# Products of 64 channels issued for two heads in turn, and pooling's outputs moved in ScalarE's order

## The chip, the cores and the metric

One core of a Trainium2 chip runs the whole program. The metric is the device time of one execution in microseconds (us), the median of three runs. A time differs from the profile's span by what lies around the span. The engines are TensorE (PE in the profile; its weight loads are PEld), VectorE (DVE), ScalarE (ACT), GpSimd (POOL) and SyncE (SP), which here only issues weight loads.

## The reference, cut to what matters

A sequence of 512 tokens with 1024 channels passes two hybrid layers (attention and retention), a feed-forward block, a token mixer, another feed-forward block and a last norm, all in fp32. The change lies in the token mixer. It has four groups of 256 channels: pooling, two gated linear attentions (`hgrn` and `gla`) and an RWKV-7 recurrence, the last three with four heads of 64 channels:

```
o = einsum('bhts,bhsv->bhtv', scores, vc) + (q * exp(b)) @ S        # hgrn, gla, per head
S_t = S_{t-1} diag(w_t) - (S_{t-1} kk_t)(kk_t * a_t)^T + v_t k_t^T  # rwkv, per head
y_pool = (window means - p) @ w_pool                                # 64 channels per window
```

## The kernel before, in words

Each engine has its own program, written out by hand in one order (`tensor_engine`, `vector_engine`, `scalar_engine`, `gpsimd_engine`, `sync_engine`). They meet through semaphores: `p.up(name, ...)` signals, `wait_ge(*of(name, ...))` waits. An engine runs its queue strictly in order, so a waiting instruction holds all that is behind it.

Features lie on partitions. The channels of head h are rows 0 to 63 (h even) or 64 to 127 (h odd) of feature tile h // 2 (`head_tile`). A product over one head's 64 channels thus has 64 rows on one half of TensorE's array: for each of four token tiles (`TT`), a 64x128 stationary and a 64x128 moving operand give a 128x128 block of one PSUM bank. TensorE takes the eight banks in turn (`take`), and waits until the reader of what was last in a bank has released it; a bank in `held` is passed over.

**Linear attention** (`linear_attention`, for `hgrn`, then `gla`). VectorE sums the log decays ("decay summed"). TensorE makes the near products k2 x q2 for the four heads, masked by VectorE. Then come nine levels in `ORDER` (32, 16, 8, 4, 2, 1, 64, 128, 256): VectorE makes log factors, ScalarE exponentials (`factor`), VectorE factors, TensorE score products (`scores`). Up to level 64 these products go by both row halves in turn already (L789). For 128 and 256 they were issued head by head, and ScalarE evicts them ("far"). Between the levels `fill(n)` issues work that doesn't depend on them: projections by weight units, whose halves ScalarE (`w_high`) and VectorE (`w_low`) split ahead of use.

**Pooling.** GpSimd makes the windows; TensorE's four pooling products are in `fill(0)` of `hgrn`. ScalarE evicts them to `y_pool`, in its own `fill(0)`, behind two weight splits. ScalarE's order was `factor(0)`, then `fill(0)`. Four banks are held by the `hgrn` values at that time, so the near products go to the four banks that pooling's outputs leave.

**The RWKV inverse** (`inverse`). When the operands are ready ("rE"), `gram` makes for each head the products AT (bI x kkE) and X (kkE x bI). Between them stand `bonus_sums` (products with 2 moving columns, into one held bank) and `turn_operands` (transposes of a token tile). VectorE masks AT and copies into XT and X, then runs `finish_gla`, the norm of gla's output, whose root ScalarE takes ahead of its inverse work. Then the inverse doubles its blocks over sizes 2, 4, 8, 16 and 32: Pm = CT x X for each head (CT by GpSimd), evicted by ScalarE, then `updates`, added to X and XT by VectorE. Between them three slots for each size take a step of `side_products`: A_ak, M_rk, M_rb (`gram` again, masked by VectorE) and Gv = A_ak x values (evicted by ScalarE). `side_products` exists on TensorE, VectorE and ScalarE, and the three must agree in their steps.

`keep_busy` issues unread products on TensorE ahead of some waits. An fp32 product stands in the trace as two records, so sixteen products are x32. Many small products go through the helper `group` and so have line L432.

## Time and profile before

| | us |
|---|---|
| three runs | 1779.49, 1781.59, 1781.84 |
| median | 1781.59 |
| profiled execution, its own time | 1780.97 |
| span of that execution | 1779.2 |
| mean granted clock over the span | 0.98 |
| mixer part up to the end of the inverse | about 960 to 1311 of the span |

The profile is of one execution. Engines are "busy" while an instruction runs; the end of a matmul is modelled and contains a tail, so the spacing of starts tells more than a duration. PEclk is the granted clock of TensorE as a share of full speed, 2.4 GHz; 0.50 is its lower level, 1.2 GHz. In brackets behind a row stands how long the engine had been idle and what released it.

### The profile page before, as it was taken

How to read it: one execution, taken by the hardware profiler on the slowest of the kernel's cores; microseconds unless marked ns; L12 is line 12 of the kernel's file. 1: busy time of each engine (PE TensorE's matmuls, PEld its weight loads, DVE VectorE, ACT ScalarE, POOL GpSimd, SP SyncE). 2: the span in 40 equal slices, each digit the busy share in tenths (PEclk: the TensorE clock that was granted, in tenths of full speed). 3: DMA queues.
4: the chain of work that ended last, by engine and by line, in shares of the span. 5: the costliest groups of instructions: out<-in, count | busy, mean ns of one | idle time of the engine just before them, and what ended most of it. 6: DMA issues, size and time to landing. Idle time of an engine off the chain costs nothing.

```text
span 1779.2 us, 22284 instructions
## 1 busy us (share of the span) xinstructions
PE 1716.0 (96%) x8770; PEld 1396.2 (78%) x8770; DVE 875.6 (49%) x1169; ACT 675.5 (38%) x1017; POOL 129.3 (7%) x126
## 2 busy tenths in 40 slices
PE   7999999999999899999999899989998899999997
PEld 6777778878778788888888688868987688888886
DVE  5633445633445565444334676765345554444333
ACT  5145564225555333333223553463132433333221
POOL 0001002001000100000002200001320200000000
PEclk9999999999999999999999899987999999999998
DMA  5422213322212233233333222100011223223331
GB/s 187 129 71 72 83 48 97 120 92 84 71 61 73 70 107 95 95 100 96 96 96 134 71 63 68 60 19 1 1 30 36 83 90 100 95 98 96 91 98 57
DMA packets 40745, 143.92 MB, mean 81 GB/s; under 512 B 4816, under 2 KB 4832, under 8 KB 40384
## 3 DMA queue, kind: packets, MB, share of 16 engines
q1 hardware_dynamic: 37008, 130.87, 22.9%
q0 software_dynamic: 2192, 8.73, 1.6%
q10 hardware_dynamic: 1440, 2.88, 0.4%
q8 instruction: 70, 1.15, 0.3%
q14 instruction: 35, 0.29, 0.1%
HBM read 140.37 MB, written 2.10 MB: 80 GB/s over the span
## 4 chain that ended last, share of the span: by engine, by line
PE 84%; DVE 10%; ACT 4%; issue 1%; DMA 0%; POOL 0%; DVEq 0%; ACTq 0%; SPq 0%
PE bank L450 23%; PE bank L451 22%; PE bank L452 22%; PE bank L432 8%; PE bank L438 2%; DVE sb_w_low L1133 2%; PE bank L789 1%; DVE sb_rot L1133 1%; PE bank L668 1%; PE bank L647 1%; PE bank L604 1%; DVE sb_xg_low L1141 1%; ACT sb_w_high L1872 1%; DVE sb_x L1133 1%; PE bank L527 0%
## 5 line engine op out<-in xcount | busy, mean ns | idle before, releaser
L1133 DVE TENSOR_TENSOR sb_w_low<-sb_raw,sb_w_high 128x1024 fp32r<-128x1024 f32 (+1 forms) x253 | 310.0, 1225 | 390.0 <-ACT sb_w_high L1872 384.0
L450 PE MATMUL bank<-sb_xg_high,sb_w_high 128*128 128x512 f32 x1176 | 468.1, 398 | 23.5 <-DVE sb_xg_low L1141 15.6
L451 PE MATMUL bank<-sb_xg_low,sb_w_high 128*128 128x512 f32 x1176 | 460.8, 392 | 0.0
L452 PE MATMUL bank<-sb_xg_high,sb_w_low 128*128 128x512 f32 x1176 | 460.8, 392 | 0.0
L1872 ACT ACTIVATE sb_w_high<-sb_raw 128x1024 fp32r<-128x1024 f32 (+1 forms) x253 | 263.4, 1041 | 354.7 <-PE bank L452 324.2
L450 PEld LDWEIGHTS bank<-sb_xg_high,sb_w_high 128*128 128x128 f32 x1176 | 222.4, 189 | 89.2 <-issue 31.0
L452 PEld LDWEIGHTS bank<-sb_xg_high,sb_w_low 128*128 128x128 f32 x1176 | 222.4, 189 | 47.7
L451 PEld LDWEIGHTS bank<-sb_xg_low,sb_w_high 128*128 128x128 f32 x1176 | 222.6, 189 | 44.3
L452 PE MATMUL bank<-sb_h_high,sb_w_low 128*128 128x512 f32 x352 | 136.9, 389 | 0.0
L450 PE MATMUL bank<-sb_h_high,sb_w_high 128*128 128x512 f32 x352 | 136.9, 389 | 0.0
L451 PE MATMUL bank<-sb_h_low,sb_w_high 128*128 128x512 f32 x352 | 136.9, 389 | 0.0
L2440 POOL TENSOR_TENSOR sb_square_sum<-sb_square_sum,sb_square 128x512 f32<-128x512 f32 x34 | 45.3, 1333 | 958.3 <-ACT sb_square L1872 882.2
L450 PE MATMUL bank<-sb_w_high,sb_xg_high 128*128 128x512 f32 x256 | 103.9, 406 | 0.5 <-DVE sb_w_low L1133 0.4
L451 PE MATMUL bank<-sb_w_low,sb_xg_high 128*128 128x512 f32 x256 | 100.6, 393 | 0.0
L452 PE MATMUL bank<-sb_w_high,sb_xg_low 128*128 128x512 f32 x256 | 100.3, 392 | 0.0
L451 PEld LDWEIGHTS bank<-sb_h_low,sb_w_high 128*128 128x128 f32 x352 | 66.1, 188 | 13.8
L452 PEld LDWEIGHTS bank<-sb_h_high,sb_w_low 128*128 128x128 f32 x352 | 66.1, 188 | 13.8
L450 PEld LDWEIGHTS bank<-sb_h_high,sb_w_high 128*128 128x128 f32 x352 | 66.1, 188 | 13.5
L1872 ACT ACTIVATE sb_h_high<-sb_up 128x512 fp32r<-128x512 f32 x44 | 27.8, 633 | 118.4 <-DVE sb_up L1133 118.4
L1133 DVE TENSOR_TENSOR sb_up<-bank,sb_inv_rms 128x512 f32<-128x512 f32 x44 | 30.4, 692 | 81.2 <-PE bank L452 80.6
L1872 ACT ACTIVATE sb_gate<-sb_gate 128x512 f32<-128x512 f32 x44 | 27.8, 633 | 95.2 <-DVE sb_gate L1133 95.2
L450 PEld LDWEIGHTS bank<-sb_w_high,sb_xg_high 128*128 128x128 f32 x256 | 48.5, 189 | 19.2 <-issue 8.2
(336 smaller groups left out, 2110.1 us busy)
## 6 DMA issues: line engine op xcount, KB each, us to landing
sb_raw<-w_ffn_in SPq DMA_DIRECT2D x88, 512.0 KB, 3.3
sb_raw<-w_ffn_out SPq DMA_DIRECT2D x32, 512.0 KB, 3.5
sb_raw<-w_tok SPq DMA_DIRECT2D x24, 512.0 KB, 3.9
sb_raw<-w_mix_f SPq DMA_DIRECT2D x18, 512.0 KB, 3.3
sb_raw<-w_rot SPq DMA_DIRECT2D x16, 512.0 KB, 3.7
sb_raw<-w_qk SPq DMA_DIRECT2D x16, 512.0 KB, 3.3
sb_raw<-w_out SPq DMA_DIRECT2D x16, 512.0 KB, 3.3
sb_raw<-w_ffn_out SPq DMA_DIRECT2D x16, 384.0 KB, 3.1
```

The lines of the kernel that those rows point to most:

```text
L432: made = e.matmul(out, lhsT, rhs, start=n == 0, stop=n == len(pairs) - 1)
L438: made = e.transpose(banks[i][:, blk(n)], in_, mem.ident)
L450: e.matmul(out, w[0], v[0], start=first, stop=False)
L451: e.matmul(out, w[0], v[1], start=False, stop=False)
L452: return e.matmul(out, w[1], v[0], start=False, stop=last)
L604: made = e.matmul(out[k], m.feat["rk"][r, f, blk(j)], m.feat["rq"][r, f, j * P:], start=part == 0, stop=part == 1)
L647: e.matmul(out[k], m.qT[r, j, blk(q)], m.kT[r, j, 0:keys], start=True, stop=True).then_inc(*p.up("scores", n, 2 * j + k, q))
L668: made = e.matmul(out[64 * k:64 * k + 64, blk(q)], m.tok["av"][:, key, h * ATT_DIM:(h + 1) * ATT_DIM], m.probT[:, 2 * (q % 2) + k, blk(key ...
L789: made = e.matmul(banks[i][:, at:at + 64].rearrange("p (n c) -> p n c", c=size), et, halves(et, size, True), start=True, stop=True)
L1133: e.tensor_tensor(out, a, b, op).then_inc(*v.up(*signal))
L1872: e.activation(out, in_, func, bias=bias, scale=scale, accum_out=accum).then_inc(*a.up(*signal))
L2440: e.tensor_tensor(out, a, b, op).then_inc(*g.up(*signal))
```

## The change

TensorE's products over one head's 64 channels are issued for two heads in turn (`HEAD_PAIRS`), one on the upper and one on the lower rows, each into its own bank; both banks are taken first. That holds for the near products, the far levels 128 and 256, and all of `gram`. In the entry to the inverse the order becomes AT of two heads, two bonus sums, X of two heads, two bonus sums, two turns. The side products get five steps for two heads (ten in all) instead of three for one (twelve in all), on all three engines. On ScalarE `hgrn`'s `fill(0)` goes ahead of `factor(0)`.

```diff
 # TensorE, linear_attention
             fill(0)
-            for h in HEADS:
-                r, g = head_tile(h)
-                i = take(("near", name, h), ("near", name, h))
-                p.wait_ge(*of("decay summed", name, 1))
+            p.wait_ge(*of("decay summed", name, 1))
+            for two in HEAD_PAIRS:
+                out = [take(("near", name, h), ("near", name, h)) for h in two]
                 for t in range(TT):
-                    group(banks[i][:, blk(t)], [(k2[r, g, blk(t)], q2[r, g, blk(t)])], "near product", name, h)
+                    for h, i in zip(two, out):
+                        r, g = head_tile(h)
+                        made = e.matmul(banks[i][:, blk(t)], k2[r, g, blk(t)], q2[r, g, blk(t)], start=True, stop=True)
+                        if t == TT - 1:
+                            made.then_inc(*p.up("near product", name, h))
...
-                    for h in HEADS:
-                        r, g = head_tile(h)
-                        i = take(("pairs", name, n, h), ("far", name, n, h))
...
+                    for two in HEAD_PAIRS:
+                        out = [take(("pairs", name, n, h), ("far", name, n, h)) for h in two]
+                        for k in range(2):
+                            for h, i in zip(two, out):
...
 # TensorE, inverse
-        def gram(what, h, left, right):
+        def gram(what, two, left, right):
...
             for t in range(TT):
-                group(banks[i][:, blk(t)], [(left[r, f, blk(t)], right[r, f, blk(t)])], what + " product", h)
+                for h, i in zip(two, out):
+                    r, f = head_tile(h)
+                    made = e.matmul(banks[i][:, blk(t)], left[r, f, blk(t)], right[r, f, blk(t)], start=True, stop=True)
...
-        for h in HEADS:
-            gram("AT", h, m.bI, m.kkE)
-            if h < 2:
-                bonus_sums(2 * h)
-            gram("X", h, m.kkE, m.bI)
-            if h < 2:
-                bonus_sums(2 * h + 1)
-            if h:
-                turn_operands(h - 1)
-        turn_operands(3)
+        for two in HEAD_PAIRS:
+            gram("AT", two, m.bI, m.kkE)
+            if not two[0]:
+                bonus_sums(0)
+                bonus_sums(1)
+            gram("X", two, m.kkE, m.bI)
+            if not two[0]:
+                bonus_sums(2)
+                bonus_sums(3)
+            for t in two:
+                turn_operands(t)
...
+            for two in HEAD_PAIRS:
+                gram("A_ak", two, m.kI, m.kkE)
+                yield
+                for h in two:
...
+                    per_tile(("Gv product", h), ("Gv", h), tile_of(m.A_ak[:, h % 2, :]),
+                             lambda t: m_tokB(t, v_cols), cols64)
+                    yield
+                gram("M_rk", two, m.kI, m.rE)
+                yield
+                gram("M_rb", two, m.bI, m.rE)
                 yield
 # ScalarE, linear_attention
-            factor(0)
-            fill(0)
+            if name == "hgrn":
+                fill(0)
+                factor(0)
+            else:
+                factor(0)
+                fill(0)
```

## Rows read from the trace of the kernel before

**Rows 1.** The page, section 1: busy time, share of the span, number of records
```profile
PE 1716.0 (96%) x8770; PEld 1396.2 (78%) x8770; DVE 875.6 (49%) x1169; ACT 675.5 (38%) x1017; POOL 129.3 (7%) x126
```

**Rows 2.** Windows by stage: stretch, length, busy (records) by engine, PEclk, DMA share, GB/s
```profile
1012.18:1024.61 12.43, 12.43 (x56) 10.52 (x57) 8.30 (x10) 4.44 (x5) 0.00 (x0) 0.65 0.31 92
...
1024.61:1167.97 143.36, 143.35 (x997) 119.48 (x996) 102.06 (x114) 65.64 (x75) 0.00 (x0) 1.00 0.20 64
...
1208.98:1232.68 23.70, 23.70 (x112) 21.85 (x113) 11.01 (x14) 5.41 (x10) 2.54 (x2) 0.57 0.00 0
...
1236.03:1311.28 75.25, 75.25 (x625) 71.83 (x625) 28.34 (x53) 14.43 (x27) 29.99 (x24) 1.00 0.00 1
```

**Rows 3.** Timeline, TensorE, pooling's products to hgrn's second scores: start, us, form, xrecords [wait]
```profile
1003.28 1.93 PE L432 MATMUL bank<-sb_window,sb_pool_w 64*64 64x512 f32 x8
...
1012.18 5.13 PE L432 MATMUL bank<-sb_kq_hgrn 64*128 64x128 f32 x32 [6.97 <-ACT sb_y_pool L1872]
...
1024.61 2.00 PE L789 MATMUL bank<-sb_E 64*128 64x64 f32 x32
...
1032.21 2.00 PE L789 MATMUL bank<-sb_E 64*128 64x64 f32 x32
```

**Rows 4.** Timeline, TensorE: hgrn's far, gla's near, lora, and gla's far products
```profile
1079.80 3.74 PE L432 MATMUL bank<-sb_E 64*128 64x128 f32 x32
...
1109.03 2.82 PE L432 MATMUL bank<-sb_kq_gla 64*128 64x128 f32 x32
...
1170.93 3.65 PE L432 MATMUL bank<-sb_mixed,sb_lora 64*128 64x512 f32 x8 [2.94 <-ACT sb_mixed L1872]
...
1191.87 1.99 PE L432 MATMUL bank<-sb_E 64*128 64x256 f32 x12 [1.26 <-DVE sb_bI L1141]
```

**Rows 5.** Timeline, ScalarE, from the logarithms to the y_pool evictions
```profile
1002.60 1.28 ACT L1872 ACT_TABLE_LOAD   x1
...
1007.84 1.06 ACT L1872 ACTIVATE sb_E<-sb_E 128x1024 f32<-128x1024 f32 x1 [3.95 <-DVE sb_E L1133]
...
1011.35 3.38 ACT L1872 ACTIVATE sb_y_pool<-bank,sb_small,sb_cols 64x512 f32<-64x512 f32 x4
```

**Rows 6.** Timeline, VectorE, same stretch: decay sums, first log factors, two splits
```profile
1003.87 2.48 DVE L1153 TENSOR_TENSOR_SCAN sb_c_hgrn<-sb_mixer,sb_c_hgrn 128x512 f32<-128x512 f32 x2
...
1006.39 1.42 DVE L1133 TENSOR_TENSOR sb_E<-sb_c_hgrn 128x512 f32<-128x512 f32 x2
...
1010.10 2.56 DVE L1133 TENSOR_TENSOR sb_w_low<-sb_raw,sb_w_high 128x1024 fp32r<-128x1024 f32 x2 [2.29 <-ACT sb_w_high L1872]
```

**Rows 7.** Timeline, TensorE, inverse: a side product block and the update behind it
```profile
1241.58 1.16 PE L432 MATMUL bank<-sb_kkE,sb_kI 64*128 64x128 f32 x8
...
1242.66 1.11 PE L432 MATMUL bank<-sb_Pm,sb_XT 128*128 128x64 f32 x8
```

**Rows 8.** Timeline, entry to the inverse: bonus products, VectorE, ScalarE's root, first update
```profile
1210.07 0.61 PE L432 MATMUL bank<-sb_mixer,sb_sigma 128*128 128x2 f32 x4
...
1210.46 0.69 DVE L1133 TENSOR_TENSOR sb_AT<-bank,sb_mixer 128x512 f32<-128x512 f32 x1 [1.53 <-ACT sb_XT L1872]
...
1211.18 0.73 DVE L1719 COPY_PREDICATED sb_XT<-sb_mixer,bank 128x512 f32<-128x512 int32 x1
...
1230.27 1.23 DVE L1133 TENSOR_TENSOR sb_square<-sb_y_gla 128x1024 f32<-128x1024 f32 x1
...
1231.53 1.22 DVE L1149 TENSOR_REDUCE sb_small<-sb_square 128x16 f32<-128x1024 f32 x1
...
1235.07 0.22 ACT L1872 ACTIVATE sb_small<-sb_small 128x16 f32<-128x16 f32 x1
...
1236.03 1.11 PE L432 MATMUL bank<-sb_Pm,sb_XT 128*128 128x64 f32 x8 [1.39 <-ACT sb_Pm L1872]
```

**Rows 9.** Windows, as rows 2, of the entry to the inverse at low clock
```profile
1212.08:1229.32 17.24, 17.24 (x74) 15.65 (x74) 6.42 (x9) 2.39 (x4) 1.87 (x2) 0.50 0.00 0
...
1229.32:1232.56 3.24, 3.24 (x16) 3.24 (x16) 2.99 (x3) 1.58 (x3) 0.00 (x0) 0.50 0.00 0
```

More of the change, by code:

```diff
@@ L39 @@
 HEADS = range(4)
+HEAD_PAIRS = ((0, 1), (2, 3))
 LAYERS = 2
@@ L793, in scores @@
                 else:
-                    for h in HEADS:
-                        r, g = head_tile(h)
-                        i = take(("pairs", name, n, h), ("far", name, n, h))
-                        if size == 128:
-                            for k, key in enumerate((0, 2)):
-                                group(banks[i][:, blk(k)], [(x2[r, g, blk(key)], x2[r, g, blk(key + 1)])],
-                                      "pairs", name, n, h)
-                        else:
-                            for key in range(2):
-                                group(banks[i][:, key * 256:(key + 1) * 256],
-                                      [(x2[r, g, blk(key)], x2[r, g, 256:512])], "pairs", name, n, h)
+                    for two in HEAD_PAIRS:
+                        out = [take(("pairs", name, n, h), ("far", name, n, h)) for h in two]
+                        for k in range(2):
+                            for h, i in zip(two, out):
+                                r, g = head_tile(h)
+                                if size == 128:
+                                    made = e.matmul(banks[i][:, blk(k)], x2[r, g, blk(2 * k)], x2[r, g, blk(2 * k + 1)],
+                                                    start=True, stop=True)
+                                else:
+                                    made = e.matmul(banks[i][:, k * 256:(k + 1) * 256], x2[r, g, blk(k)],
+                                                    x2[r, g, 256:512], start=True, stop=True)
+                                if k:
+                                    made.then_inc(*p.up("pairs", name, n, h))
                 p.mark("factors read", name, n)
@@ L923, in inverse @@
         before_products = ("rE",)
-        def gram(what, h, left, right):
-            r, f = head_tile(h)
-            i = take((what, h), {"AT": ("XT made", 2, h), "X": ("X made", 2, h)}.get(what, (what, h)))
+        def gram(what, two, left, right):
+            out = [take((what, h), {"AT": ("XT made", 2, h), "X": ("X made", 2, h)}.get(what, (what, h))) for h in two]
             p.wait_ge(*of(*before_products))
             for t in range(TT):
-                group(banks[i][:, blk(t)], [(left[r, f, blk(t)], right[r, f, blk(t)])], what + " product", h)
+                for h, i in zip(two, out):
+                    r, f = head_tile(h)
+                    made = e.matmul(banks[i][:, blk(t)], left[r, f, blk(t)], right[r, f, blk(t)], start=True, stop=True)
+                    if t == TT - 1:
+                        made.then_inc(*p.up(what + " product", h))
         def per_tile(key, freed_by, left, right, out):
@@ L1729, in side_products @@
         def side_products():
-            for h in HEADS:
-                if h >= 2:
-                    v.wait_ge(*of("Gv product", h - 2))
-                masked("A_ak", m.A_ak[:, h % 2, :], h, mem.table("before"))
+            for two in HEAD_PAIRS:
+                for h in two:
+                    if h >= 2:
+                        v.wait_ge(*of("Gv product", h - 2))
+                    masked("A_ak", m.A_ak[:, h % 2, :], h, mem.table("before"))
                 yield
-                masked("M_rk", m.M_rk[:, h, :], h, mem.table("upto"))
                 yield
-                masked("M_rb", m.M_rb[:, h, :], h, mem.table("upto"))
+                yield
+                for h in two:
+                    masked("M_rk", m.M_rk[:, h, :], h, mem.table("upto"))
+                yield
+                for h in two:
+                    masked("M_rb", m.M_rb[:, h, :], h, mem.table("upto"))
                 yield
@@ L2151, in scores @@
                     act(m.far[:, h, at], bank("pairs", name, n, h)[:, 0:at.stop - at.start], "far", name, n, h)
[L2153 to L2154 removed]
+            if name == "hgrn":
+                fill(0)
+                factor(0)
+            else:
+                factor(0)
+                fill(0)
             for n in range(len(ORDER)):
@@ L2321, in side_products @@
         def side_products():
-            for h in HEADS:
+            for two in HEAD_PAIRS:
                 yield
-                a.wait_ge(*of("Gv product", h))
-                a.wait_ge(*of("y made", "gla"))
-                act(m.Gv[:, h, :], bank("Gv product", h)[:, 0:TT * 64], "Gv", h)
+                for h in two:
+                    a.wait_ge(*of("Gv product", h))
+                    a.wait_ge(*of("y made", "gla"))
+                    act(m.Gv[:, h, :], bank("Gv product", h)[:, 0:TT * 64], "Gv", h)
+                    yield
                 yield
```

11 lines of the change are left out of this document (3 added, 8 removed).

## The prediction

> **What bounds the kernel now.** The page first: TensorE is busy 1716.0 us of 1779.2 [rows 1], so time can be won only where TensorE's own work gets shorter, where it waits, or where its clock is low. The change touches the mixer part alone, so I cut that part into stages [rows 2]. TensorE is busy for 143.35 of 143.36 us between the first score products of hgrn and the last of gla; it is bound by its own work there, and what comes out of it, or ahead of it, comes off the end. The entry to the inverse (1208.98 to 1232.68) is also full of matmuls, at a mean clock of 0.57; the inverse behind it runs at 1.00 without a gap. The stretch before the first scores (to 1024.61) has 0.65.
>
> The timeline of TensorE says why: behind pooling's products it stands idle for 6.97 us, released by ScalarE's eviction of y_pool, and the 16 near products of hgrn then take 5.13 us [rows 3], where gla's 16 of the same shape take 2.75 [rows 4]. ScalarE's queue gives the reason for the wait: table load, then an exponential that waits for VectorE until 1007.84, then two weight splits in the 2.45 us before 1011.35, and only there the y_pool evictions [rows 5], though pooling's products began at 1003.28.
>
> **Part 1, pooling ahead of the exponents.** The change puts two splits and four evictions ahead of the first exponential on ScalarE. Their inputs are there: the logarithms end at about 1002.5 (the load starts then). The two splits fill at most 2.45 us: to 1004.9. Evictions at 3.38/4 = 0.85 each: the second ends at 1006.6, the fourth at 1008.3. The near products of heads 0 and 1 now take two banks at once, so they need the second eviction, and the decay sums, which end at 1006.35 [rows 6]. They start at 1006.6 and take 1.0; heads 2 and 3 go from 1008.3 to 1009.3. Behind them TensorE needs the next weight unit. VectorE's low halves wait behind its first log factors (1006.39 + 1.42), then 1.28 for the first: 1009.1. So the unit starts at 1009.3, where it started at 1017.3. At full clock a unit takes 5.6 us (the score products at 1024.61 and 1032.21 stand 7.6 apart, with 2.0 of their own and one unit between [rows 3]), and the scores would begin at 1014.9.
>
> What is queued behind: the table load (1.28) now falls after the evictions, the exponential ends at 1010.7 instead of 1008.9, VectorE's factors at 1012.0, its near copies after that. None is late for scores at 1014.9. SP only sees its weight loads released about a microsecond earlier; POOL has no part. The DMA queues are at 0.20 share there [rows 2].
>
> The clock: it fell in the 6.97 us wait. Now the waits are 1.3 and 0.7 us, but around them stand only pooling's quarter-array products and a microsecond of near products. I expect a short fall all the same, for most of a unit: nearly what the unit lost before (7.3 us from 1017.3 to 1024.6, against 5.6), 1.5 us; bounds 0 and 3.5. Part 1 gives 1024.61 - 1014.9 - 1.5 = **8.2 us** (6.2 to 9.7).
>
> **Part 2, two heads in turn.** No row shows these products alternated at 128 columns, so I bound one pair. From above: 16 products of 64 rows with 64 moving columns, already alternated (L789), take 2.00 us [rows 3]: 0.25 a pair, loads of 128 stationary columns included. Also alternated are four lora products of 512 columns, at half clock: 3.65 us [rows 4]. hgrn's near products at that clock take 5.13/13 = 0.39 for 128 columns, so one of 512 needs 1.6 and four in a row 6.3: two and two ran together. From below: gla's near products, four at a time on one row half, take 2.75/13 = 0.21 each if each of the three changes of half hides one product (2.75 is to the next start; the row's 2.82 has the tail). A pair at 0.21 to 0.25 costs what one product costs now. The worst end is no gain (rival 2).
> Here the Trainium skill speaks against the change: "TensorE: Matmul & The Clock Gate", Part 3, says that a weight load overlaps running matmuls only if the row group differs. By it a half would load, stream, then load again, 0.43 a pair, and the sum below would lose nearly all of part 2. The trace disagrees: four products of one half follow each other in 1.08 us [rows 7], 0.27 each, not 0.43, so the sum does not use it.
>
> Priced so:
> - gla's near products: 2.75 to 1.9, gain **0.8**; TensorE-bound, so all of it counts.
> - hgrn's far products: 8 of 128 and 8 of 256 columns take 3.66 us to the next start (the row of rows 4 merges both sizes and has the tail); four pairs of each take 0.85 + 1.7 + 0.4 for starts = 2.95: gain **0.7**.
> - gla's far products: heads 0 and 1 now both wait for the bank that VectorE frees at 1191.87 [rows 4]; ScalarE's four evictions then come in a row instead of one early, and the exponentials behind them are on VectorE's path to rE: about half an eviction of the length in rows 5, loss **0.4**.
> - inverse side products: 12 blocks of 1.08 become 6 [rows 7]. **Gain 6.5**, if no wait takes their place. With none of them, VectorE, ScalarE and POOL must keep up with products and updates alone; the stage is 38% VectorE, 19% ScalarE, 40% POOL [rows 2], and two heads in turn give each copy at least one block of TensorE's time. I take no wait; bound 2 us lost.
>
> **Part 3, the entry to the inverse.** Before, from first product (1208.98) to the first update (1236.03) [rows 8] is 27.05 us. After, at full clock: AT of two heads 1.1, four bonus products 1.0 (two take 0.54), X of two heads 1.1, bonus 1.0, two turns of operands 1.8 (16 transposes took 3.24 at half clock [rows 9]), AT 1.1, X 1.1, turns 1.8: TensorE is through after 10 us. So the cover is gone and the wait changes hands. VectorE needs per head a mask (0.72) and two predicated copies (0.84 with the step to the next) [rows 8]. AT of heads 2 and 3 is there at 7.4 us; VectorE finishes six operations 4.8 us later, at 12.2; then finish_gla's squares and reduction (1.26 each) to 14.7; ScalarE's root, which is ahead of Pm in its queue, starts at 15.0, its table load done earlier; the first update followed the root's start by 0.96 [rows 8], with Pm of head 0 between: 16.0, say 16.1. The first Pm product also waits, since seven banks turn round, for the XT copy of head 3 at 11.4. The stage takes 16.1 instead of 27.05: gain 10.9, less 0.5 for a chance of a low clock during the bonus products: **10.4**.
>
> **The price of it.** TensorE now stands idle for about 1.3 and then 2.8 us with 1.9 us of work between. In the trace a wait of 6.97 us cost the clock, and so did plain thin work: it fell in this very stage, with no wait, and stayed at 0.50 for 17.24 us of one-half products and transposes; it came back only at the end of 3.24 us of nothing but transposes [rows 9]. So I expect the inverse to begin at 1.2 GHz. It came back behind the transposes, and behind the alternated lora products of rows 4. The nearest to these in the inverse is a Pm product next to a pair of side products (3.7 us at half clock), or two Pm products. The first such stretch comes after updates of two heads and a product (3.5 + 1.8 + 3.5 us), so the half clock lasts about 12 us and costs **6** (0 if it never falls; 13 if the first stretch misses).
>
> **Sum.** 8.2 + 0.8 + 0.7 - 0.4 + 6.5 + 10.4 - 6 = 20.2 us. The profiled execution took 1780.97 us for its span of 1779.2; that gives 1760.8. The median of the runs is 0.6 higher, 1761.4. The last term has its tail on the dear side, so I say 1762. Terms at their good ends: 9.7 + 1.1 + 6.5 + 10.9 = 28.2, or 1753. At their bad ends: 6.2 + 1.1 + 4.5 + 9.5 - 13 = 8.3, or 1773.
>
> **Rivals.**
> 1. The clock holds through the entry, or comes back at once. For it: the pairs fill both halves of the array, where the trace fell on one-half products. Against: the 2.8 us wait. Sum without the last term, 26.2: 1755. Chance 0.15.
> 2. The change doesn't do what it says: pairs don't overlap at 128 columns, because each half waits for its own loads. Then part 1 gives 8.2, part 2 nothing, and part 3, with products as long and a clock as low as now, little: 1773. For it: the four products of rows 7 take 1.08, a little over 4 x 0.21. Against: rows 3 and 4. Chance 0.05. (This is what the page's rule above would give.)
> 3. The low clock stays for 25 to 45 us of the inverse, since most of it is 64-column updates that wait on loads: cost 13 to 22, time 1768 to 1777. For it: the 17 us at 0.50. Against: the stretch is at 1.00 now with the same updates. Chance 0.15.
> 4. Slower: the low clock lasts through the inverse. Its place is the idle before the first update; about 69 us of work would take 69 more, 26.2 is won elsewhere: 1824. It decides from 52 us of half clock on, where the cost (half the time) passes 26.2. Against it: two stretches like that in each of five sizes. Chance 0.03.
> The forecast itself: 0.62.
>
> **Chances.** A measurement of this kernel can tell about 0.2%, 3.6 us, from no change. Faster by more than that needs a time under 1778: forecast, rivals 1 and 2, nearly all of 3: 0.94. Between: the rest of 3 and a bad rival 2: 0.03. Slower: 0.03. The range that holds 8 in 10 leaves out rival 4, the slow part of 3 and the fastest of 1: 1752 to 1773.
>
> **What would show it.** hgrn's near products beginning 3.3 us after pooling's first product instead of 8.9, the table load behind y_pool; gla's 16 near products in about 1.9 us; side blocks of 16 records in 1.1 to 1.2 us, six of them; a first update 16 us after the first AT product with VectorE and ScalarE, not TensorE, before it; and a granted clock below 1 for the first 12 us of the inverse. Wrong if a pair costs more than 0.3 us, if the Pm evictions begin to hold TensorE in the inverse, or if the clock in the inverse is low for more than one size.

## The result, and the profile after

The changed kernel took 1755.63 us, median of four runs (1755.07 to 1756.98), beside 1780.54 for the kernel before on the same chip (1779.12 to 1781.84). The ratio is 0.9861, 95% interval 0.9844 to 0.9878. The forecast was 1762, range 1752 to 1773. The profiled execution took 1755.07 us for a span of 1753.3.

The starts of the same work on TensorE in both traces give the account. "Foretold" is the prediction's own term, all numbers are us.

| TensorE reaches | before | after | won in the step | foretold |
|---|---|---|---|---|
| pooling's products | 1003.28 | 1003.27 | 0.0 | 0 |
| hgrn's first scores | 1024.61 | 1016.94 | 7.7 | 8.2 |
| hgrn's far products | 1079.80 | 1073.68 | -1.6 | 0 |
| gla's near products | 1109.03 | 1102.96 | -0.1 | 0.7 |
| gla's last 64-channel scores | 1164.20 | 1157.66 | 0.5 | 0.8 |
| first AT product | 1208.98 | 1203.08 | -0.6 | -0.4 |
| first update | 1236.03 | 1218.81 | 11.3 | 10.4 |
| end of the inverse | 1311.28 | 1288.31 | 5.8 | 6.5 - 6 |
| end of the recurrence | 1384.65 | 1358.71 | 3.0 | 0 |
| end of the span | 1779.2 | 1753.3 | 0.0 | 0 |

The sum won is 25.9 us against 20.2 foretold. Two places make the difference: the inverse (5.8 for 0.5) and the recurrence (3.0 for nothing). These are two single executions, and that of the changed kernel is the fastest of its four; by the medians the change is worth 24.9 us in this set and 22.4 in a second set further down.

The page's first section, which answers to [rows 1], shows where it went: TensorE's busy time fell by 22.7 us, on the same number of records.

```profile
PE 1693.3 (97%) x8770; PEld 1377.0 (79%) x8770; DVE 875.3 (50%) x1169; ACT 674.9 (38%) x1017; POOL 129.9 (7%) x126
```

**Ahead of the first scores.** ScalarE's timeline, which answers to [rows 5]:

```profile
1002.78 2.23 ACT L1891 ACTIVATE sb_w_high<-sb_raw 128x1024 fp32r<-128x1024 f32 x2
1005.12 3.37 ACT L1891 ACTIVATE sb_y_pool<-bank,sb_small,sb_cols 64x512 f32<-64x512 f32 x4
1008.57 1.28 ACT L1891 ACT_TABLE_LOAD   x1
1009.87 1.06 ACT L1891 ACTIVATE sb_E<-sb_E 128x1024 f32<-128x1024 f32 x1
```

TensorE's timeline beside it, which answers to [rows 3] (rows left out are weight-unit products):

```profile
1003.27 1.93 PE L433 MATMUL bank<-sb_window,sb_pool_w 64*64 64x512 f32 x8
1006.91 1.16 PE L780 MATMUL bank<-sb_kq_hgrn 64*128 64x128 f32 x16 [1.70 <-ACT sb_y_pool L1891]
1008.64 1.73 PE L780 MATMUL bank<-sb_kq_hgrn 64*128 64x128 f32 x16 [0.57 <-ACT sb_y_pool L1891]
1010.31 0.79 PE L451 MATMUL bank<-sb_w_high,sb_xg_high 128*128 128x512 f32 x1
...
1016.94 0.55 PE L793 MATMUL bank<-sb_E 64*128 64x64 f32 x6
```

The wait of 6.97 us is now 1.70 and 0.57. The second block of the same form takes 1.73 us where the first took 1.16: the clock fell within it, and the first row of the weight unit, 0.79 (0.50 for the first row of the next unit, at full clock), shows it low still. The last row shown is cut by the end of the view: it is the start of 32 records.

**The entry to the inverse.** Rows that answer to [rows 8], TensorE first:

```profile
1203.08 1.16 PE L938 MATMUL bank<-sb_kkE,sb_bI 64*128 64x128 f32 x16 [0.19 <-DVE sb_rE L1147]
1204.18 1.05 PE L433 MATMUL bank<-sb_mixer,sb_sigma 128*128 128x2 f32 x8
1205.16 1.16 PE L938 MATMUL bank<-sb_bI,sb_kkE 64*128 64x128 f32 x16
1206.25 1.05 PE L433 MATMUL bank<-sb_mixer,sb_sigma 128*128 128x2 f32 x8
...
1214.18 2.02 PE L433 MATMUL bank<-sb_X,sb_CT 128*128 128x128 f32 x16 [1.19 <-DVE sb_XT L1733]
1218.81 1.11 PE L433 MATMUL bank<-sb_Pm,sb_XT 128*128 128x64 f32 x8 [2.60 <-ACT sb_Pm L1891]
```

VectorE's timeline from the last XT copy on, then ScalarE's up to the first Pm evictions:

```profile
1213.31 0.72 DVE L1733 COPY_PREDICATED sb_XT<-sb_mixer,bank 128x512 f32<-128x512 int32 x1
...
1215.34 1.22 DVE L1147 TENSOR_TENSOR sb_square<-sb_y_gla 128x1024 f32<-128x1024 f32 x1
1216.59 1.22 DVE L1163 TENSOR_REDUCE sb_small<-sb_square 128x16 f32<-128x1024 f32 x1
```
```profile
1217.85 0.22 ACT L1891 ACTIVATE sb_small<-sb_small 128x16 f32<-128x16 f32 x1 [1.89 <-DVE sb_small L1163]
1218.15 1.28 ACT L1891 ACTIVATE sb_Pm<-bank 128x512 f32<-128x512 f32 x2
```

This is the hand-over that the prediction drew: TensorE is through with the operands after 10 us, and then the bank of head 3's XT, VectorE's reduction, ScalarE's root and the Pm eviction behind it set the first update.

How much of the 11.3 us is what? Windows over the entry of before, then of after (columns as in [rows 2]):

```profile
1208.98:1236.03 27.05, 25.65 (x129) 23.61 (x129) 11.76 (x16) 8.39 (x15) 4.58 (x4) 0.62 0.00 1
```
```profile
1203.08:1218.81 15.73, 11.94 (x129) 10.99 (x129) 11.81 (x16) 8.39 (x15) 5.80 (x4) 1.00 0.01 2
```

At a mean clock of 0.62, 27.05 x 0.38 = 10.3 us of before's busy time were the price of the clock. Without it TensorE had 15.4 us of work; now it has 11.9. Waits rose from 1.4 to 3.8. So 11.3 = 10.3 (clock) + 3.4 (shorter work) - 2.4 (more waiting). By this account the gain is nearly all clock. The two traces don't say which part of the change kept the clock up, the alternation or the new order of the blocks; the experiment with the alternation undone bears on it.

**The inverse.** A side block of two heads, which answers to [rows 7], on TensorE's timeline; then windows over the whole inverse [rows 2] and over its one low stretch:

```profile
1225.99 1.16 PE L938 MATMUL bank<-sb_kkE,sb_kI 64*128 64x128 f32 x16
```
```profile
1218.81:1288.31 69.50, 69.50 (x624) 67.25 (x624) 28.13 (x53) 14.41 (x27) 29.80 (x24) 0.98 0.01 1
...
1220.70:1224.10 3.40, 3.40 (x18) 3.40 (x17) 1.68 (x3) 0.60 (x1) 1.27 (x1) 0.50 0.00 0
```

Eight products of two heads, alternated, take 1.09 us to the next start; four of one head took 1.08. TensorE is busy all through; no eviction took the place of the work removed. The half clock that I expected for 12 us lasted 3.4.

### The profile page after: what moved, and what is told of

Same layout as the page of the kernel before. It is cut to its first block, busy times and chain, and to the rows that moved or that the text cites. A ratio compares the mean times of both kernels' runs of the same rounds, so it can differ in the third digit from the quotient of the medians.

```text
span 1753.3 us, 22293 instructions
## 1 busy us (share of the span) xinstructions
PE 1693.3 (97%) x8770; PEld 1377.0 (79%) x8770; DVE 875.3 (50%) x1169; ACT 674.9 (38%) x1017; POOL 129.9 (7%) x126
## 4 chain that ended last, share of the span: by engine, by line
PE 81%; DVE 12%; ACT 5%; issue 1%; DMA 0%; POOL 0%; DVEq 0%; ACTq 0%; SPq 0%
PE bank L451 23%; PE bank L452 22%; PE bank L453 22%; PE bank L433 6%; DVE sb_w_low L1147 2%; PE bank L439 2%; ACT sb_w_high L1891 1%; PE bank L669 1%; PE bank L648 1%; PE bank L605 1%; DVE sb_xg_low L1155 1%; DVE sb_E L1147 1%; PE bank L793 1%; DVE sb_x L1147 1%; DVE sb_rot L1147 1%
## 5 line engine op out<-in xcount | busy, mean ns | idle before, releaser
L451 PE MATMUL bank<-sb_xg_high,sb_w_high 128*128 128x512 f32 x1176 | 469.1, 399 | 23.8 <-DVE sb_xg_low L1155 15.4
L451 PEld LDWEIGHTS bank<-sb_h_high,sb_w_high 128*128 128x128 f32 x352 | 66.1, 188 | 13.7
L452 PEld LDWEIGHTS bank<-sb_h_low,sb_w_high 128*128 128x128 f32 x352 | 66.1, 188 | 13.7
L453 PEld LDWEIGHTS bank<-sb_h_high,sb_w_low 128*128 128x128 f32 x352 | 66.1, 188 | 13.7
```

The costliest lines, as they stand in the source:

```text
L451: e.matmul(out, w[0], v[0], start=first, stop=False)
L452: e.matmul(out, w[0], v[1], start=False, stop=False)
L453: return e.matmul(out, w[1], v[0], start=False, stop=last)
```

## The experiments

Times are medians. Where kernels ran with the same "before" they are named together.

### Pooling's order alone, and the pairs alone

The first is the kernel before with only ScalarE's order changed, the second the changed kernel with only that undone:

```diff
-            factor(0)
-            fill(0)
+            if name == "hgrn":
+                fill(0)
+                factor(0)
+            else:
+                factor(0)
+                fill(0)
```

> The kernel before with only ScalarE's order changed (hgrn's fill(0) ahead of factor(0)). Theory (the first near products waited only for the y_pool evictions, and the wait cost the clock): the first score products of hgrn start 7 to 8 us earlier than before, near 1017, and the whole is 7 to 9 us shorter than before, 1772 to 1774. Rival A (the wait only changes hands, to the weight split or the exponential): first scores after 1022, whole within 3 us of before.

> The changed kernel with ScalarE's old order. Theory (the two parts add up): 7 to 8 us above the changed kernel, 1762 to 1764. Rival A (the order gives nothing once products alternate): within 2 us of the changed kernel, 1754 to 1758.

Measured: 1770.89 (1768.77 to 1772.38) and 1760.12 (1759.37 to 1762.32), before 1778.85; ratios 0.9958 (0.9943 to 0.9973) and 0.9897 (0.9881 to 0.9914). TensorE, near products of hgrn, of the order alone, then of the pairs alone:

```profile
1006.39 3.96 PE L432 MATMUL bank<-sb_kq_hgrn 64*128 64x128 f32 x32 [1.28 <-DVE sb_c_hgrn L1153]
```
```profile
1013.59 0.80 PE L780 MATMUL bank<-sb_kq_hgrn 64*128 64x128 f32 x4 [7.85 <-ACT sb_y_pool L1891]
```

By the medians the order is worth 8.0 us by itself. By head, only the first bank is needed, so the products start on the decay sums (1.28), not on the second eviction. Without it the pairs wait 7.85 us, 0.9 more than before, because two evictions must be done. The two parts sum to 8.0 + 18.7 = 26.7 against 24.9 and 22.4 for both in the two sets of the changed kernel. That is 2 to 4 us too much, and the second expectation missed by as much: the pairs alone lie 4.5 and 3.4 us above the two sets, not 7 to 8. The starts on TensorE are steadier than the medians. From pooling's products to the first AT product the kernel before takes 205.7 us and the order alone 199.4, so the order wins 6.3 there; the pairs alone take 206.5 and the changed kernel 199.8, so it wins 6.7 on top of the pairs. In that stretch the two parts add up. (The first expectation had 7 to 8 us for it and 1772 to 1774 for the whole; the first scores came 6.4 us earlier, at 1018.24, and the median is 1.1 below the range.) The rest of the medians lies where the order changes nothing: the trace of the order alone has no low clock in the recurrence, where that of the kernel before has two stretches of 3.4 us.

### Alternation undone, order kept

Each block still holds two heads, but head by head. The cut shows `gram`; the near and the far products are edited in the same way:

```diff
-            for t in range(TT):
-                for h, i in zip(two, out):
-                    r, f = head_tile(h)
+            for h, i in zip(two, out):
+                r, f = head_tile(h)
+                for t in range(TT):
```

> The changed kernel with the same blocks, banks and steps, but in each block all products of one head, then all of the other. Theory (two products on different row halves run at the same time): each side block of 16 records takes 1.9 to 2.1 us instead of 1.09, six of them 5 to 6 us; the near products together 1 us more; the entry to the inverse falls to the low clock or at least takes 4 to 8 us longer. Whole 1767 to 1772. Rival B (the gain is in the grouping: fewer changes between half-row and full-row products, fewer steps): within 3 us of the changed kernel.

Measured: 1774.04, ten runs from 1761.65 to 1776.35, before 1778.85; ratio 0.996 (0.9938 to 0.9981). The profiled run is the fastest of the ten. Its timeline on TensorE, gla's near products and a side block:

```profile
1103.08 2.88 PE L780 MATMUL bank<-sb_kq_gla 64*128 64x128 f32 x32
1105.89 0.50 PE L451 MATMUL bank<-sb_w_high,sb_xg_high 128*128 128x512 f32 x1
...
1231.84 1.71 PE L938 MATMUL bank<-sb_kkE,sb_kI 64*128 64x128 f32 x16
1233.48 0.33 PE L433 MATMUL bank<-sb_Pm,sb_XT 128*128 128x64 f32 x1
```

A side block of two heads takes 1.64 us by head, 1.09 alternated, and two blocks of one head took 2 x 1.08. So of the 1.07 us that a merged block saves, half (0.55) is alternation and half (0.52) is one block less to start and end. The expectation had 1.9 to 2.1 us for the block, which would have left almost nothing to this second half. That also prices products of one row half at 1.64/8 = 0.21 when they run on, as the prediction had from gla's near products.

The profiled run is 6.6 us above the changed kernel's. The shorter products account for about 6 of that: 0.55 for each of the six side blocks, as much at most for each of the four entry blocks, and 0.5 for gla's near products. That the rest is so small is luck of two traces: this one loses 1.7 us more to the clock in the entry and as much in the inverse, and wins 2.6 behind the recurrence, where the changed kernel's clock falls once more. The other nine runs lie up to 14.7 us above that, at a mean granted clock down to 0.976 where the fastest run has 0.988. The longer runs have the lower clock, so with the products by head it is low longer in most executions. Where, I can't show: the trace is of the fastest run. Alternation is thus worth about 6 us in products and, by the medians (18.4 us apart), some 12 more, which go with the clock.

The same trace says something of the entry to the inverse. Its window, from the first AT product to the first update:

```profile
1204.57:1223.03 18.46, 15.44 (x129) 14.50 (x129) 11.77 (x16) 8.39 (x15) 5.78 (x4) 0.91 0.00 1
```

The clock is low for 3.4 us there, not for the 20.5 us of the kernel before, and the entry takes 18.5 us, not 27.05: in this execution 8.6 of the 11.3 us came with the new order of the blocks alone. The order alone on ScalarE, whose entry is as before, has the 20.5 us again. So in the entry it was not the alternation that kept most of the clock, at least in the fastest of these ten runs. What it does in the other nine is open, and no run has the old order of blocks with alternated products.

### The far levels by head

```diff
-                    for two in HEAD_PAIRS:
-                        out = [take(("pairs", name, n, h), ("far", name, n, h)) for h in two]
...
+                    for h in HEADS:
+                        r, g = head_tile(h)
+                        i = take(("pairs", name, n, h), ("far", name, n, h))
...
```

> The changed kernel with only the levels 128 and 256 issued head by head again. Theory (there, taking two banks ahead makes TensorE wait for ScalarE's evictions, 0.59 us in hgrn, and delays the exponentials of rwkv by 0.3 us in gla, which gives back what alternating won): hgrn's far products take 3.6 to 3.8 us as in the changed kernel, the whole is within 1 us of it, 1754.6 to 1756.2. Rival C (alternating them is worth 0.7 us or more): 1756.5 or above.

Measured: 1764.73 (1755.11 to 1766.58), before 1778.85; ratio 0.9913 (0.9884 to 0.9943). TensorE, hgrn's far products, by head:

```profile
1071.43 3.74 PE L433 MATMUL bank<-sb_E 64*128 64x128 f32 x32
1075.10 0.50 PE L451 MATMUL bank<-sb_w_high,sb_xg_high 128*128 128x512 f32 x1
```

and of the changed kernel, TensorE, then ScalarE's four evictions of level 128 (0.45 us each; the second ends just before TensorE goes on at 1075.43):

```profile
1073.68 1.16 PE L804 MATMUL bank<-sb_E 64*128 64x128 f32 x16
1075.43 2.08 PE L807 MATMUL bank<-sb_E 64*128 64x256 f32 x16 [0.59 <-ACT sb_far L1891]
1077.44 0.50 PE L451 MATMUL bank<-sb_w_high,sb_xg_high 128*128 128x512 f32 x1
```
```profile
1074.42 1.81 ACT L1891 ACTIVATE sb_far<-bank 128x256 f32<-128x256 f32 x4 [1.58 <-PE bank L804]
```

3.67 us by head, 3.76 in pairs: no gain. Both banks are taken before the first product of a pair, and the bank comes free only with ScalarE's eviction; the 0.59 us wait eats what the pairs save.

In gla the pairs even lose. From the lora products to the first AT product it is 38.0 us by head (here, in the kernel before and in the order alone) and 38.6 in pairs (in both traces of the changed kernel, in the pairs alone and in three more; in the remaining five the clock falls once more at about 1185, and it is 39.4 to 39.7). So the far levels are better left by head, by 0.6 us.

The expectation of the whole, within 1 us of the changed kernel, missed by 8. The 9 us that the median is above the changed kernel's do not come from there: counted from pooling's products the first AT product comes 0.7 us earlier than in the changed kernel's trace. The windows behind the first update, which stands at 1217.62, show what happened instead:

```profile
1218.00:1245.50 27.50, 27.50 (x137) 27.05 (x137) 7.03 (x13) 3.41 (x7) 5.07 (x4) 0.50 0.00 1
1245.50:1288.00 42.50, 42.50 (x405) 41.45 (x405) 17.74 (x36) 8.53 (x15) 15.24 (x12) 1.00 0.01 1
```

About 27.4 us at half clock, 13.7 lost, on the same code that lost 1.7 in the changed kernel's trace. This is the mechanism of rival 3, met in another kernel, behind the same 2.60 us wait for Pm. Whether the far levels by head have a part in it is open; one of its four runs took 1755.11, as the changed kernel.

### The changed kernel again, and the two waits of the entry taken away

Unchanged; then ScalarE's root behind the first two Pm evictions:

```diff
-        finish_gla()
...
+            if size == 2:
+                finish_gla()
```

then also the turn of the banks moved on by three behind the bonus sums, so that the first Pm product meets a bank that is free:

```diff
+        turn[0] += 3
```

> The changed kernel itself, more executions. Theory (the 2.6 us wait before the first update leaves the clock low in the inverse, and how long it stays low differs from execution to execution): times in two groups, some at 1753 to 1757, some 6 to 12 us above, at a lower mean clock. Rival D (only the form of the far products made the slow executions of the fourth run): all within 1754 to 1758.

> The changed kernel with ScalarE's finish_gla (table load and root) behind its first two Pm evictions instead of ahead of them. Theory (the first update waits for Pm of head 0, which waits in ScalarE's queue for the root and so for VectorE): the wait before the first update falls from 2.6 us to under 1, the first update comes about 13.3 us after the first AT product instead of 15.7; the low clock in the inverse gets rarer. Median 1750 to 1754. Rival E (something else holds the first update, the XT copies or a bank): first update still after 15 us or more, time as the changed kernel.

> As the run before, and TensorE passes over three banks ahead of the first Pm product, so that this takes a bank that ScalarE has emptied and not the one that waits for the XT copy of head 3. Theory: the 1.2 us wait ahead of the first Pm product goes too, first update about 12 us after the first AT product, no wait over 1 us is left in the entry and the clock holds there. Median 1749 to 1752, hardly any execution above 1755. Rival F (the X and XT copies on VectorE then hold the updates themselves): the gain over the run before is under 0.5 us.

> The kernel with the root behind the first Pm evictions and the bank turn moved on by three, once more. Its earlier four runs lay from 1748.8 to 1758.2 and those of the changed kernel from 1752.7 to 1761.9. Theory (two waits, 3.8 us together, are gone from the entry, nothing else is changed but the luck of the clock): median 1750 to 1754, first update 12.3 us behind the first AT product, as before. Rival (the lower median of the earlier runs was luck, the time is set behind the entry): 1755 to 1758, no different from the changed kernel.

Measured: changed again 1756.75 (1752.66 to 1761.88); root moved 1754.29 (1746.74 to 1757.96); root and bank 1751.09 (1748.81 to 1758.18), before 1779.15, ratios 0.9875 (0.9858 to 0.9893), 0.9858 (0.9837 to 0.9878) and 0.9849 (0.983 to 0.9868). Root and bank again: 1752.47 (1751.13 to 1757.81), before 1778.23, ratio 0.9855 (0.9828 to 0.9882). TensorE's first update with the root moved, then with both:

```profile
1214.14 2.02 PE L433 MATMUL bank<-sb_X,sb_CT 128*128 128x128 f32 x16 [1.20 <-DVE sb_XT L1733]
1216.00 1.06 PE L433 MATMUL bank<-sb_Pm,sb_XT 128*128 128x64 f32 x8
```
```profile
1211.31 1.95 PE L433 MATMUL bank<-sb_X,sb_CT 128*128 128x128 f32 x16
1213.83 1.11 PE L433 MATMUL bank<-sb_Pm,sb_XT 128*128 128x64 f32 x8 [0.57 <-ACT sb_Pm L1892]
```

From the first AT product (1203.04 and 1201.56) that is 12.96 and 12.27 us (12.27 again in the repeated set), against 15.73. Rivals E and F are out: both waits were where the prediction put them, the root costs 2.8 us, the bank 0.7. Of the 3.5 us about that much arrives in the median: all eight runs of the changed kernel have the median 1755.98, the eight of root and bank 1752.25 (on different chips, their kernels before within 2.3 us). The groups overlap, and so do the intervals, so this version is probably, not surely, better than the changed kernel; it beats the kernel before by 28.1 and 25.8 us in its two sets.

The expectations on the clock did less well. The changed kernel's second set has one run at 1761.88 and three from 1752.66 to 1757.28: rival D, all within 1754 to 1758, is out, so times above that don't need the far products by head, but one run is no group. With the root moved the low clock did not get rarer: three of the four traces that have it, without a filled wait, show 10.2 us at half clock in the inverse, where both traces of the changed kernel show 3.4. And "hardly any execution above 1755" missed: one of four is at 1758 in each set of root and bank.

### Unread products in the waits

The changed kernel with three unread products behind the first Pm products, where TensorE waits 2.60 us:

```diff
             product(0)
             product(1)
+            if size == 2:
+                keep_busy(3)
```

> The changed kernel with three unread products of 512 columns on TensorE in its 2.6 us wait before the first update; nothing else moves. Theory (it is the idle time that costs the clock): the granted clock stays at 1.00 through the inverse, no execution is above 1757, median 1752 to 1755. Rival G (the thin work behind the wait brings the clock down whatever stands in the wait): low clock in the inverse as before, executions at 1761 to 1767 remain.

Measured: 1753.70 (1751.30 to 1755.03, five runs), before 1779.15; ratio 0.9854 (0.9841 to 0.9868). TensorE's timeline at that place, and the window over the inverse:

```profile
1214.79 2.74 PE L751 MATMUL bank<-sb_inv_rms,sb_ones 128*128 128x512 f32 x6
1217.56 1.11 PE L433 MATMUL bank<-sb_Pm,sb_XT 128*128 128x64 f32 x8
```
```profile
1215.00:1287.00 72.00, 71.98 (x644) 67.95 (x643) 31.57 (x59) 15.89 (x31) 32.55 (x25) 1.00 0.01 1
```

The clock stays at 1.00 over the whole inverse, and the spread is 3.7 us, against 9.2 in the changed kernel's second set. But its first set of four had spread over only 1.9, so the spread says little. The clear sign is the clock behind this wait: low in all six traces that have the 2.60 us idle, not low here. That fits the idle as the cause of the fall there, on one trace.

The same with one product (0.9 us) in the 0.57 us wait of root and bank:

```diff
+            if size == 2:
+                keep_busy(1)
```

> The kernel of the run beside it, with one unread product of 512 columns (0.9 us) in the last wait before the first update (0.57 us, released by ScalarE's first Pm eviction). Theory (the idle costs the clock in the inverse): no low clock between the first AT product and the end of the inverse, a smaller spread of times, median within 2 us of its neighbour, 0.4 us lost in the entry. Rival (the fall comes from the thin half-row products of the entry, idle or not): low clock stretches in the inverse as often as in the neighbour's runs, spread 5 us or more.

Measured: 1754.09 (1752.24 to 1755.66), beside 1752.47 for its neighbour; ratio 0.9866 (0.9842 to 0.9891). No low clock between the first AT product and the end of the inverse in its trace, spread 3.4 us against 6.7. The theory's signs are there, and the median is 1.6 us above its neighbour's, within the 2 us foretold. Against them stands how little idle can go before a fall: three of the four traces with the root moved and no filled wait behind it have half clock for 10.2 us from about 1226 on, with no wait over 0.66 us in the 10 us ahead of the fall. The fourth, which is the first of the two traces of root and bank, has none. And in the entry of the kernel before the clock fell with no wait at all. Two traces with filled waits and no fall are too few to call the idle the cause here; that it is likely is all that the runs give.

### An unread filling of the other wait

TensorE waits 3.03 us for ScalarE's tanh ahead of gla's lora products, and the clock is low from 1162.8 to 1179.6 in the changed kernel, longer than before (3.4 us, a gap, 6.8). Three unread products in that wait, in the changed kernel and on top of root and bank:

```diff
         def operand_steps():
             yield
+            keep_busy(3)
```

> The changed kernel with one edit ahead of the inverse: three unread products of 512 columns (2.8 us at full clock) are issued where TensorE waits 3.03 us for ScalarE's tanh, ahead of gla's lora products. In the changed kernel the clock falls at the start of that wait and stays at 1.2 GHz for 17 us, while the kernel before had 10. Theory (the idle costs the clock there, as in the wait before the first update): clock 1.00 from 1161 to 1180, TensorE's 15.8 us of work between the wait and the size-128 products shrink by 5 to 7.5, the first AT product starts 4 to 7 us earlier than 1203.1 (VectorE's chain to rE, 10.7 us busy of those 15.8, takes the rest), time 1750 to 1753. Rival A (plain thin work, the 64-column score products before it, costs the clock, with or without the wait): low clock as before, time 1756 to 1758. Rival B (VectorE's chain, not TensorE, sets the start of the first AT product): clock 1.00, but the first AT product less than 1.5 us earlier, time 1755 to 1757.

> The changed kernel with the root behind the first Pm evictions, the bank turn moved on by three, and the three unread products ahead of gla's lora products. The two waits before the first update are gone (4.9 us less in the entry, as measured), and by the theory the low clock ahead of the inverse too (4 to 7 us). Theory: first AT product at 1196 to 1199, first update 12.3 us behind it, time 1743 to 1748, about 10 below the changed kernel. If thin work costs the clock there whatever stands in the wait: 1750 to 1752, as without the unread products.

Measured: 1761.38 (1760.11 to 1763.05) and 1757.62 (1753.52 to 1758.11), before 1781.06; ratios 0.9898 (0.9883 to 0.9913) and 0.9867 (0.985 to 0.9883). Neither is faster than without it: the theory missed by 8 us and more, and the medians lie about 5 us above the kernels that they extend, of which up to 3 may be the chip, whose kernel before is that much slower. The intervals of the ratios overlap for the second, and for the first with one of the two sets of the changed kernel. TensorE's timeline of the first:

```profile
1159.49 2.84 PE L751 MATMUL bank<-sb_inv_rms,sb_ones 128*128 128x512 f32 x6
1162.64 1.99 PE L433 MATMUL bank<-sb_mixed,sb_lora 64*128 64x512 f32 x8 [0.31 <-ACT sb_mixed L1892]
...
1168.78 3.68 PE L793 MATMUL bank<-sb_E 64*128 64x64 f32 x32 [2.28 <-DVE sb_near L1546]
...
1183.68 3.33 PE L807 MATMUL bank<-sb_E 64*128 64x256 f32 x16 [2.11 <-DVE sb_bI L1156]
...
1202.07 1.16 PE L939 MATMUL bank<-sb_kkE,sb_bI 64*128 64x128 f32 x16 [0.20 <-DVE sb_rE L1148]
```

The lora products run at full clock, 1.99 us instead of 3.78, as the idle theory says. Then TensorE waits for VectorE: 2.28 us for a predicated copy, where the clock falls after all (mean 0.52 from 1168.78 to 1177.63), and 2.11 for bI, where it had waited 1.29. This execution is 1.9 us ahead of the changed kernel's already at pooling's products, so I count from there. bI then releases TensorE 182.3 us in, as in the changed kernel (182.2), although the clock was low for 10.2 us between and not for 17.1: up to bI, VectorE's chain sets the stage, which is the mechanism of rival B. The three kernels with the far products by head say the same, with 10.2, 13.7 and 17.1 us of half clock and 38.0 us from lora to AT in each. TensorE's slow clock costs next to nothing there. Rival B's signs did not all come: the clock was not 1.00, and the time is 4 us over its 1757.

The loss lies behind bI. The clock falls once more at 1184.2, the 256-column products take 3.33 us for 2.00, and the first AT product comes 0.9 us later than in the changed kernel. In the inverse there are 10.2 us at half clock (1218.3 to 1228.6; 3.4 in the changed kernel), which cost 3.2 us more, and the recurrence takes 2.8 us more, as in the changed kernel's second trace. Why the fall behind the same 2.60 us wait lasts longer here is open, and so is whether the unread products have a part in it.

## Why the prediction was right, and where it was off

The waits and the shorter products came as drawn, and the time lay in the range, 6.4 us under the point. On the clock the forecast was not right: it came back almost at once, which is rival 1, given a chance of 0.15, whose 1755 the time met. Part of that meeting is luck: 3.0 of the 25.9 us between the two traces come from a stage that the change doesn't touch. By the steps of the prediction:

- **Part 1.** 7.7 for 8.2. The near products began 3.64 us behind pooling's first product (3.3 foretold), the table load stood behind y_pool, and the short fall of the clock came (3.4 us). Not foretold: a second fall of 3.4 us behind gla's gate products, 1036.3 to 1039.8, where the trace of before has none; it takes the 1.6 us of the next step. It seems to belong to the first: the two traces of root and bank, one kernel, show 3.4 us at the start and 3.4 here, and 6.8 at the start and none here. Most other traces are of one of these two kinds, but not all: the pairs alone have 10.2 and 3.4, the filled wait none and 3.4. Together the two falls cost 3.4 us in the changed kernel, which is the 3.5 that the prediction gave as bound of its 1.5. The window, as [rows 2]:

```profile
1033.00:1041.00 8.00, 8.00 (x41) 5.66 (x39) 5.58 (x8) 2.48 (x4) 0.00 (x0) 0.79 0.22 68
```

- **A pair costs what one product did.** Right: four pairs take 1.09 us to the next start, 0.27 a pair, where four products of one head took 1.08. So the second half of the array is free. With the start of its block a pair is a little over the 0.25 of the estimate. Here the trace had spoken against the Trainium skill ("TensorE: Matmul & The Clock Gate", Part 3), by which a load overlaps running matmuls only for another row group (the same part also has loads into the background weight buffer pulled ahead). Eight products, four on each half one after the other, take 1.64 us, 0.21 each; that leaves hardly any room for a load that waits for the product ahead of it. By which way the load is hidden no run here shows. Rival 2 fell with the 1.09.
- **gla's near products.** 2.30 us, not 1.9: gain 0.45, not 0.8. The 1.9 is eight pairs at 0.21 to 0.25 in one run; in fact the two heads' four pairs are a block, and each of the two blocks has its own start. The weight loads show it, 0.20 us between the two blocks:

```profile
1102.96 0.97 PEld L780 LDWEIGHTS bank<-sb_kq_gla 64*128 64x128 f32 x16 [0.35 <-issue]
1104.13 1.00 PEld L780 LDWEIGHTS bank<-sb_kq_gla 64*128 64x128 f32 x16 [0.20 <-issue]
```

- **hgrn's far products.** 0 for 0.7. The prediction costed two banks at once for gla and for pooling, but not here; the wait for ScalarE's evictions (0.59) is what it overlooked. gla's far products: -0.6 for -0.4, and the experiment by head shows the 0.6.
- **The entry.** 15.73 us for 16.1, with every wait in its place (root 14.8 us in for 15.0). What it had not said is that 10.3 of the 11.3 us won are clock, so that the whole step hung on its own words "at full clock". Its allowance for a low clock there was 0.5 us, and its reason, under rival 1, that pairs fill both halves of the array. In the trace with the alternation undone the clock is low for only 3.4 us in the entry, so the new order of the blocks may be the better reason.
- **Side blocks.** Six of 1.09 for twelve of 1.08: 6.4 for 6.5. The inverse won 5.8 us and lost 1.7 of clock, so about one more is unexplained: fewer changes between kinds of block may have given it, which no run shows by itself.
- **The price of the clock.** This is the term that was off most: "the half clock lasts about 12 us and costs 6". It fell where foretold, after the 2.60 us wait, and lasted 3.4 us: 1.7. It is not a constant of the kernel: profiled runs of kernels with the same 2.60 us wait show 3.4, 3.4, 3.4, 6.8, 10.2 and 27.3 us. In the first three the fall began 1.5 to 2.0 us behind the first update, in the others within 0.6 us of it. The forecast's 12 is inside that scatter, 3.4 is the commonest; a range was right, a likeliest value of 12 was not, and I took it from where the clock had come back in one trace.
- **The recurrence.** 3.0 us that no step named. It has the same waits for y_rwkv (0.9 and 1.7 us) before and after. In the trace of before the clock fell at two of them, in this one at none, and in the changed kernel's second trace it fell twice, at 1318 and 1335. The fourteen traces have 0, 3.4 or 6.8 us of half clock there, and that of the order alone, with TensorE's program as before, has none. So the 3.0 us are luck of single executions; an account from two traces must leave a few us to it.

## What to carry to other kernels

Products that use half of TensorE's rows should be issued for two operands in turn, on either half: with 128 fp32 columns the second was free here. Merge their blocks too, since half of the gain of a merged block came from the start that it saves, and take both banks only where the reader of the old content is ahead: where it wasn't, pairs won nothing (hgrn's far products) or lost 0.6 us (gla's). Then read the granted clock by stage before pricing anything: here one stage's clock (0.62 to 1.00) was worth as much as all the shortened products, and a slow clock in a stage that another engine sets cost next to nothing. Compare starts by stage, counted from a common point: the fourteen traces differ by up to 2.7 us at pooling's products, up to which all programs are the same, and by 3 in the recurrence.

## What the runs showed of the hardware that was not expected

- How long a low clock lasts differs between executions of one kernel and between near-twins: behind the same wait of 2.60 us it was at 1.2 GHz for 3.4 to 27.3 us.
- With the products by head, ten runs of one kernel spread over 14.7 us, at mean clocks of 0.976 to 0.988; alternated, eight runs spread over 9.2, and with the entry's wait filled 3.7. The products by head alone don't make the spread: thirteen runs of the kernel before, on the same chip, spread over 3.8.
- The entry to the inverse was at half clock for 20.5 us in both traces with the old order of its blocks, with no wait between its first product and the fall. In the twelve with the new order it was for 3.4 us (with the alternation undone, and with the far levels by head) or not at all.
- Filling one wait moved the fall to the next one instead of removing it (from 1161 in the changed kernel's second trace to 1167), and the stretch in the inverse got longer. More products issued did not mean a clock that stays up.
